# The pause of TensorE in the second unit of every segment: the wait moved one matmul forward, ahead of the next one

## The chip, the cores and the metric

The kernel runs on one core of a Trainium2 chip. The metric is the time of one execution on the device in microseconds (us), the median of several runs. Everything is computed in one launch.

## The reference

Two blocks follow one another on 256 tokens of width 2048. Nearly all of the work is in projections, which multiply the activations by weights of 2048 rows.

```python
# first block
h = rmsnorm(x, ln_g); proj = h @ w_in                      # gMLP, delta-rule and cross-attention inputs
out_a = gmlp_spatial_gating(...) * silu(g_z)
out_b = rmsnorm(gated_delta_rule(q, k, v, g, beta)) * silu(d_z)
out_c = cross_attention(c_q, memory keys, memory values) * silu(c_z)
x = rmsnorm(x + concat(out_a, out_b, out_c) @ w_out, final_g)
# second block
h = rms_norm(x, gain); proj = h @ w_in_2
merged = sigmoid(g_a) * (stick_breaking(q_a, k_a, v_a) @ w_branch_a) \
       + sigmoid(g_b) * (forgetting(q_b, k_b, v_b) @ w_branch_b)
x = x + merged @ w_out_2
# expert layer: query, top-16 product keys per head, softmax gates, 16384 experts
x = x + sum_k gate_k * gelu(expert_u[id_k] . h) * expert_v[id_k]
out = rms_norm(x, final_gain)
```

The kernel computes the expert layer densely: in 8 chunks of 2048 experts an "up" projection by `expert_u`, a product with a dense table of gates, and a "down" projection by `expert_v`.

## The kernel before

**Units.** All projections are cut into 460 units. A unit is one block of 2048 x 128 weights (1 MB) against all 256 tokens, accumulated in one PSUM bank. It is done in two halves (h = 0, 1) of 8 tiles of 128 rows each. To keep float32 accuracy, weights and activations are split into an upper and a lower part, and each tile takes three matmuls: upper weights by upper activations, upper weights by lower activations, and lower weights by upper activations. A half is therefore three groups of 8 matmuls, and a unit is 48 matmuls with 48 weight loads. Every one of them has the shape 128x128 by 128x256.

**Who makes what.** SyncE loads the weights (`raw`, a ring of 4 units). ScalarE makes the upper part `whi` of a half (line 427), GpSimd the lower part `wlo` (line 404), TensorE multiplies (all matmuls are recorded at line 1345), ScalarE or VectorE takes the result out of PSUM. `whi` and `wlo` have 4 slots, one for each half: ScalarE may convert a half once TensorE has finished the half four before it. The activations are `xhi`, `xlo` (or `bhi`, `blo`; in the down projections `hid_upper`, `hid_lower`). The semaphores are `hi_ready`, `lo_ready` (a half is converted), `pe_half` (TensorE has finished a half) and `evac` (a bank is free).

**Segments.** TensorE's program is written as segments of 4 to 24 units, 34 in all. The first two units of a segment are written out, and the rest are in a loop of two units. Between some segments other work stands (transposes, attention, sums for the norms). Eight units at the start and the 16 units of the up projection of chunk 2, between which the gate table is built, are written without segments.

**The pause.** In the second unit of each segment (`paused` is true for j = 1) the last of the first 8 matmuls of half 0 increments a semaphore `beat` when it is finished, and TensorE itself waits for that semaphore a little later. Nobody else uses `beat`. Where `fresh` is set for this unit, which is so only in the paired segment of the branches, the group with `wlo` comes before the one with the lower activations; elsewhere the lower activations come first.

Of the kernel before, what the change touches and what calls it, by code (L numbers as in the profile page):

```python
# [29 lines left out]
HALF = KT // 2  # L30
# [78 lines left out]
def program(nc, ap, out, g_dram):  # L109
    ctx = ExitStack()  # L110
    with ctx:
# [193 lines left out]
        conv_used, beat = sem("conv_used"), sem("beat")  # L305
# [1037 lines left out]
        def _(pe):  # L1343
# [3 lines left out]
            beats = [0]  # L1347


            def pause(k, z):  # L1350
                if k == HALF - 1:
                    z.then_inc(beat, 1)
                    beats[0] += 1
                elif k == 0:
                    pe.wait_ge(beat, beats[0])

            def unit_body(u, j, hi, lo, par, paired=False, fresh=None, between=None, paused=False):

                s0 = (2 * j) % 4
                o = unit_ps[:, j % 2, :]
                if not (isinstance(par, int) and par == 0):
                    pe.wait_ge(evac[j % 2], par)
                for h in range(2):
                    def tile(k):
                        return k + HALF * (j % 2) if paired else k + HALF * h

                    def upper_x(k):
                        if fresh is not None and k % 4 == 0:  # L1370
                            pe.wait_ge(*fresh(tile(k) // 4)[0])

                    def lower_x(k):
                        if fresh is not None and k % 4 == 0:
                            pe.wait_ge(*fresh(tile(k) // 4)[1])

                    oo = o[:, h * S:(h + 1) * S] if paired else o[:, 0:S]
                    opens, closes = paired or h == 0, paired or h == 1
                    pe.wait_ge(hi_ready, u * 2 + (2 * j + h + 1))
                    for k in range(HALF):  # L1380
                        upper_x(k)
                        z = mm(oo, whi[:, s0 + h, k, :], hi[:, tile(k), :], start=opens and k == 0, stop=False)
                        if paused and h == 0 and k == HALF - 1:
                            pause(k, z)

                    def with_lower_x(stop):
                        for k in range(HALF):
                            lower_x(k)
                            z = mm(oo, whi[:, s0 + h, k, :], lo[:, tile(k), :], start=False, stop=stop and k == HALF - 1)
                            if paused and h == 0 and k == 0:  # L1390
                                pause(k, z)
                        return z

                    def with_lower_w(stop):
                        pe.wait_ge(lo_ready, u * 2 + (2 * j + h + 1))
                        for k in range(HALF):
                            z = mm(oo, wlo[:, s0 + h, k, :], hi[:, tile(k), :], start=False, stop=stop and k == HALF - 1)
                        return z

                    if fresh is not None:  # L1400
                        with_lower_w(False)
                        z = with_lower_x(closes)
                    else:
                        with_lower_x(False)
                        z = with_lower_w(closes)
                    z.then_inc(pe_half, 1)

                    if between is not None and h == 0:
                        between()
# [73 lines left out]
            for t in range(TT):  # L1483
                for h in range(XA_HEADS):
                    z = tr(psf[:, 1024 + (t * 4 + h) * P:1024 + (t * 4 + h + 1) * P], mvf[:, h, t * P:(t + 1) * P])
# [10 lines left out]
            for h in range(XA_HEADS):  # L1496
                for t in range(TT):
                    n = 2 * h + t
                    z = mm(psf[:, 1024 + n * S:1024 + (n + 1) * S], cq[:, h, t * P:(t + 1) * P], mk[:, h, :])
# [3 lines left out]
            for h in range(XA_HEADS):  # L1503
                for m in range(TT):
                    for t in range(TT):
                        z = tr(psf[:, 1024 + (2 * h + m) * S + t * P:1024 + (2 * h + m) * S + (t + 1) * P],
                               xa_p[:, 2 * h + t, m * P:(m + 1) * P])
# [4 lines left out]
            for h in range(XA_HEADS):  # L1512
                for m in range(TT):
                    z = mm(psf[:, h * S:(h + 1) * S], mvt[:, m, h, :], xa_pt[:, h, m, :], m == 0, m == TT - 1)
# [4 lines left out]
            for g in range(GROUPS):  # L1519
                z = mm(psf[:, 1024:1024 + S], ones, gv[:, g, :], g == 0, g == GROUPS - 1)  # L1520
# [9 lines left out]
            for t in range(TT):  # L1530
                for x, m in enumerate((C64_LE, C64_GT)):
                    z = mm(psf[:, 768 + (2 * t + x) * 8:768 + (2 * t + x + 1) * 8], c(m), gbt[:, t, 0, :])
            z.then_inc(sg("gsum_mm"), 1)
            pe.wait_ge(sg("ln_sq"), 1)
            for g in range(GROUPS):
                z = mm(psf[:, 1536:1536 + S], ones, vsq[:, g, :], g == 0, g == GROUPS - 1)
# [3 lines left out]
            for g in range(GROUPS):  # L1540
                for t in range(TT):
                    z = tr(psf[:, 2048 + (2 * g + t) * P:2048 + (2 * g + t + 1) * P], gv[:, g, t * P:(t + 1) * P])
# [4 lines left out]
            for g in range(GROUPS):  # L1547
                for t in range(TT):
                    o = psf[:, 1024 + (2 * g + t) * P:1024 + (2 * g + t + 1) * P]
                    z = mm(o, vt[:, g, t, :], wst[:, g, :])  # L1550
# [30 lines left out]
            for n in range(16):  # L1581
                z = tr(ps_b[:, n * P:(n + 1) * P], qkv[:, 8 + n // 2, (n % 2) * P:(n % 2 + 1) * P])
            z.then_inc(sg("k_t"), 1)
            pe.wait_ge(sg("exp_row"), 1)
            for n in range(16):
                kk = qkv[:, 8 + n // 2, (n % 2) * P:(n % 2 + 1) * P]
                z = mm(ps_a[:, n * P:(n + 1) * P], kk, kk)
# [4 lines left out]
            for n in range(16):  # L1592
                z = tr(ps_b[:, n * P:(n + 1) * P], qkv[:, 16 + n // 2, (n % 2) * P:(n % 2 + 1) * P])
            z.then_inc(sg("v_dt"), 1)
            pe.wait_ge(sg("kk_out"), 1)
            for n in range(16):
                sl = slice((n % 2) * P, (n % 2 + 1) * P)
                z = mm(ps_a[:, n * P:(n + 1) * P], qkv[:, 8 + n // 2, sl], qkv[:, n // 2, sl])
# [291 lines left out]
```

## Time and profile before

| | |
|---|---|
| median of 3 runs | 3000.95 us (2997.36 to 3005.54) |
| profiled execution, own time | 3004.29 us |
| its span, first to last instruction | 3002.5 us |
| TensorE matmuls busy | 2906.8 us, 97% |
| TensorE weight loads busy | 2865.0 us, 95% |
| GpSimd busy | 2289.1 us, 76% |
| ScalarE busy | 1312.0 us, 44% |
| VectorE busy | 1063.2 us, 35% |
| mean granted TensorE clock | 0.987 of full speed |

The busy times come from one profiled execution. Matmuls overlap one another in the records (one begins before the last has ended), so the rate of TensorE is read from the distance between starts and not from busy time.

### The profile page before, as it was taken

How to read it: one execution, taken by the hardware profiler on the slowest of the kernel's cores; microseconds unless marked ns; L12 is line 12 of the kernel's file. 1: busy time of each engine (PE TensorE's matmuls, PEld its weight loads, DVE VectorE, ACT ScalarE, POOL GpSimd, SP SyncE). 2: the span in 40 equal slices, each digit the busy share in tenths (PEclk: the TensorE clock that was granted, in tenths of full speed). 3: DMA queues.
4: the chain of work that ended last, by engine and by line, in shares of the span. 5: the costliest groups of instructions: out<-in, count | busy, mean ns of one | idle time of the engine just before them, and what ended most of it. 6: DMA issues, size and time to landing. Idle time of an engine off the chain costs nothing.

```text
span 3002.5 us, 58955 instructions
## 1 busy us (share of the span) xinstructions
PE 2906.8 (97%) x24182; PEld 2865.0 (95%) x24182; DVE 1063.2 (35%) x1558; ACT 1312.0 (44%) x1547; POOL 2289.1 (76%) x925
## 2 busy tenths in 40 slices
PE   7999979999999988999999999999999999999998
PEld 7999979899999987999999999999999999999998
DVE  6113365353000025225698981403104040033322
ACT  6355542554534343444443664343433334333333
POOL 6787730588878852888799548888888888889986
PEclk9999989999999998999999999999999999999999
DMA  6445410344545530555454555564564645655553
GB/s 241 169 175 184 162 62 0 113 176 175 194 169 196 182 140 31 193 195 183 156 182 177 215 224 210 182 219 173 192 215 180 224 168 196 219 192 205 211 188 118
DMA packets 85829, 524.37 MB, mean 175 GB/s; under 512 B 8672, under 2 KB 23136, under 8 KB 24544
## 3 DMA queue, kind: packets, MB, share of 16 engines
q1 hardware_dynamic: 68400, 489.38, 45.5%
q10 hardware_dynamic: 17328, 33.56, 3.0%
q8 instruction: 75, 1.23, 0.2%
q14 instruction: 26, 0.21, 0.0%
HBM read 504.03 MB, written 18.87 MB: 174 GB/s over the span
## 4 chain that ended last, share of the span: by engine, by line
PE 51%; POOL 23%; issue 20%; DVE 5%; POOLq 0%; ACT 0%; DVEq 0%; ACTq 0%
PE banks L1345 51%; POOL wlo L404 23%; DVE oh L1273 2%; DVE oh L1269 1%; DVE hidden L1283 1%; POOLq L403 0%; DVE T L800 0%; PE banks L1455 0%; DVE hid_lower L1316 0%; DVE dec L1007 0%; POOLq L398 0%; DVE picks L1254 0%; DVE at__97 L1015 0%; DVE qkv L967 0%; ACT expr L605 0%
## 5 line engine op out<-in xcount | busy, mean ns | idle before, releaser
L404 POOL TENSOR_TENSOR wlo<-raw,whi 128x1024 fp32r<-128x1024 f32 x920 | 2284.4, 2504 | 661.6 <-ACT whi L427 660.7
L427 ACT ACTIVATE whi<-raw 128x1024 fp32r<-128x1024 f32 x916 | 943.0, 1055 | 763.2 <-PE banks L1345 755.8
L1345 PE MATMUL banks<-xhi,whi 128*128 128x256 f32 x4928 | 681.8, 281 | 7.1 <-ACT xhi L508 7.0
L1345 PE MATMUL banks<-xhi,wlo 128*128 128x256 f32 x4928 | 678.4, 280 | 6.2 <-POOL wlo L404 6.2
L1345 PE MATMUL banks<-xlo,whi 128*128 128x256 f32 x4928 | 682.6, 281 | 1.9 <-DVE xlo L807 1.9
L1345 PEld LDWEIGHTS banks<-xhi,whi 128*128 128x128 f32 x4928 | 622.1, 189 | 9.3 <-issue 7.8
L1345 PEld LDWEIGHTS banks<-xlo,whi 128*128 128x128 f32 x4928 | 623.4, 189 | 5.8 <-DVE xlo L807 2.5
L1345 PEld LDWEIGHTS banks<-xhi,wlo 128*128 128x128 f32 x4928 | 620.9, 189 | 7.6 <-POOL wlo L404 7.6
L878 DVE TENSOR_TENSOR X<-banks,X 128x256 f32 (+1 forms) x112 | 47.5, 424 | 768.9 <-PE banks L1345 768.9
L1345 PE MATMUL banks<-hid_lower,whi 128*128 128x256 f32 x2048 | 285.5, 282 | 2.4 <-DVE hid_lower L1316 2.4
L1345 PEld LDWEIGHTS banks<-hid_lower,whi 128*128 128x128 f32 x2048 | 261.1, 190 | 3.7 <-DVE hid_lower L1316 2.6
L453 ACT ACTIVATE hidden<-banks 128x256 f32 (+1 forms) x128 | 49.4, 386 | 401.0 <-PE banks L1345 400.8
L1345 PE MATMUL banks<-hid_upper,whi 128*128 128x256 f32 x1536 | 213.1, 282 | 0.0
L1345 PE MATMUL banks<-hid_upper,wlo 128*128 128x256 f32 x1536 | 212.2, 281 | 0.0
L1345 PEld LDWEIGHTS banks<-hid_upper,whi 128*128 128x128 f32 x1536 | 195.4, 190 | 0.0
L1345 PEld LDWEIGHTS banks<-hid_upper,wlo 128*128 128x128 f32 x1536 | 194.3, 189 | 0.0
L1273 DVE TENSOR_SCALAR oh<-banks,sel 128x128 f32<-128x128 f32 x256 | 84.2, 398 | 0.0
L1310 DVE TENSOR_TENSOR hidden<-hidden,gch 128x1024 f32<-128x1024 f32 x28 | 59.2, 2114 | 60.7 <-PE banks L1345 60.7
L1345 PE MATMUL banks<-bhi,wlo 128*128 128x256 f32 x512 | 70.9, 281 | 0.7 <-POOL wlo L404 0.7
L1345 PE MATMUL banks<-bhi,whi 128*128 128x256 f32 x512 | 71.2, 282 | 0.0
L1345 PE MATMUL banks<-blo,whi 128*128 128x256 f32 x512 | 71.1, 281 | 0.0
L1345 PE MATMUL banks<-oh,oh 128*128 128x128 f32 x512 | 64.3, 282 | 4.0 <-DVE oh L1273 3.2
(352 smaller groups left out, 2156.8 us busy)
## 6 DMA issues: line engine op xcount, KB each, us to landing
raw<-in_w_exp SPq DMA_DIRECT2D x256, 1024.0 KB, 4.8
raw<-in_w_in SPq DMA_DIRECT2D x132, 1024.0 KB, 4.8
raw<-in_w_out SPq DMA_DIRECT2D x32, 1024.0 KB, 4.8
raw<-in_w_br SPq DMA_DIRECT2D x16, 1024.0 KB, 4.8
raw<-in_w_q SPq DMA_DIRECT2D x16, 1024.0 KB, 4.8
gates<-gst ACTq DMA_DIRECT2D x16, 1024.0 KB, 4.7
gch<-gates ACTq DMA_DIRECT2D x7, 2048.0 KB, 12.8
raw<-in_w_kv SPq DMA_DIRECT2D x8, 1024.0 KB, 9.5
```

The costliest lines, as they stand in the source:

```text
L404: pool.tensor_tensor(wlo[:, s, :, :], raw[:, j, h * HALF:(h + 1) * HALF, :], whi[:, s, :, :].bitcast(F32), ALU.subtract).then_inc(lo_ready, 1)
L427: act.activation(whi[:, (2 * j + h) % 4, :, :], raw[:, j, h * HALF:(h + 1) * HALF, :], ACT.Copy).then_inc(hi_ready, 1)
L453: act.activation(dst[:, bass.ds(i * RING + j, 1), :], unit_ps[:, j % 2:j % 2 + 1, 0:S], func).then_inc(evac[j % 2], 1)
L878: return dve.tensor_tensor(blk(X, i, j), unit_ps[:, j % 2:j % 2 + 1, 0:S], blk(X, i, j), ALU.add)
L1269: dve.tensor_tensor(oh2[:, b8:b8 + 8, :], iota.unsqueeze(1).broadcast_to([P, 8, P]), row.unsqueeze(2).broadcast_to([P, 8, P]), ALU.is_equa ...
L1273: dve.tensor_scalar(oh1[:, b, :], iota, col(0), col(2), ALU.is_equal, ALU.mult).then_inc(sg("oh"), 1)
L1283: dve.tensor_tensor(h, h, gst[:, g16 % 2, 0:KT, :], ALU.mult).then_inc(sg("gated_first"), 1)
L1310: dve.tensor_tensor(h4, h4, gch[:, :, ks, :].rearrange("p g a n -> p a g n"), ALU.mult).then_inc(sg("gates_used"), 1)
L1345: return nc.tensor.matmul(o, lhsT, rhs, start=start, stop=stop, **k)
```

## The change

The wait for `beat` is placed directly behind the matmul that increments it, ahead of the very next matmul. Before, one more matmul was issued in between. Nothing else differs; no other engine's program changes.

```diff
-            def pause(k, z):
-                if k == HALF - 1:
-                    z.then_inc(beat, 1)
-                    beats[0] += 1
-                elif k == 0:
-                    pe.wait_ge(beat, beats[0])
+            def pause(z):
+                z.then_inc(beat, 1)
+                beats[0] += 1
+                pe.wait_ge(beat, beats[0])
...
                     for k in range(HALF):
                         upper_x(k)
                         z = mm(oo, whi[:, s0 + h, k, :], hi[:, tile(k), :], start=opens and k == 0, stop=False)
                         if paused and h == 0 and k == HALF - 1:
-                            pause(k, z)
+                            pause(z)
 
                     def with_lower_x(stop):
                         for k in range(HALF):
                             lower_x(k)
                             z = mm(oo, whi[:, s0 + h, k, :], lo[:, tile(k), :], start=False, stop=stop and k == HALF - 1)
-                            if paused and h == 0 and k == 0:
-                                pause(k, z)
                         return z
```

TensorE's program at the pause of an ordinary segment (the up projection of chunk 0), before the change. A row is one matmul or several alike, out <- moving operand, weights; the first two rows are the 8 upper by upper matmuls.

```order
L1345 MATMUL banks<-xhi,whi 128x256 [waits hi_ready,evac1]
L1345 MATMUL banks<-xhi,whi 128x256 x7
L1345 MATMUL banks<-xlo,whi 128x256
L1345 MATMUL banks<-xlo,whi 128x256 [waits beat]
L1345 MATMUL banks<-xlo,whi 128x256 x6
L1345 MATMUL banks<-xhi,wlo 128x256 [waits lo_ready]
L1345 MATMUL banks<-xhi,wlo 128x256 x7
```

The same place of the changed kernel:

```order
L1345 MATMUL banks<-xhi,whi 128x256 [waits hi_ready,evac1]
L1345 MATMUL banks<-xhi,whi 128x256 x7
L1345 MATMUL banks<-xlo,whi 128x256 [waits beat]
L1345 MATMUL banks<-xlo,whi 128x256 x7
L1345 MATMUL banks<-xhi,wlo 128x256 [waits lo_ready]
L1345 MATMUL banks<-xhi,wlo 128x256 x7
```

The wait has moved from the second to the first of the eight matmuls behind the one that it waits for. 33 of the 34 pauses look like this one.

The one in the paired segment of the branches, before the change:

```order
L1345 MATMUL banks<-xhi,whi 128x256 [waits lin_hi]
L1345 MATMUL banks<-xhi,whi 128x256 x3
L1345 MATMUL banks<-xhi,wlo 128x256 [waits lo_ready]
L1345 MATMUL banks<-xhi,wlo 128x256 x7
L1345 MATMUL banks<-xlo,whi 128x256 [waits lin_lo2]
L1345 MATMUL banks<-xlo,whi 128x256 [waits beat]
L1345 MATMUL banks<-xlo,whi 128x256 x2
```

And the same place of the changed kernel:

```order
L1345 MATMUL banks<-xhi,whi 128x256 [waits lin_hi]
L1345 MATMUL banks<-xhi,whi 128x256 x3
L1345 MATMUL banks<-xhi,wlo 128x256 [waits lo_ready,beat]
L1345 MATMUL banks<-xhi,wlo 128x256 x7
L1345 MATMUL banks<-xlo,whi 128x256 [waits lin_lo2]
L1345 MATMUL banks<-xlo,whi 128x256 x3
```

Here nine matmuls stood between the increment and the wait, and now none does.

## Rows read from the trace of the kernel before

**Rows 1.** The page: busy time (share of the span) of each engine

```profile
PE 2906.8 (97%) x24182; PEld 2865.0 (95%) x24182; DVE 1063.2 (35%) x1558; ACT 1312.0 (44%) x1547; POOL 2289.1 (76%) x925
```

**Rows 2.** Two stretches of 76 us, matmuls of line 1345 (busy, count; loads; clock; DMA)

```profile
1190.00:1266.00 76.00, 76.00 (x673) 76.00 (x672) 1.00 0.57 205
1284.00:1360.00 76.00, 76.00 (x648) 76.00 (x647) 1.00 0.55 199
```

**Rows 3.** Matmuls in order of time about two pauses (start, length, group)

```profile
76.20 1.07 PE L1345 MATMUL banks<-xhi,whi 128*128 128x256 f32 x8
77.10 1.31 PE L1345 MATMUL banks<-xlo,whi 128*128 128x256 f32 x8
78.25 1.11 PE L1345 MATMUL banks<-xhi,wlo 128*128 128x256 f32 x8
79.19 1.11 PE L1345 MATMUL banks<-xhi,whi 128*128 128x256 f32 x8
...
1997.42 0.40 PE L1345 MATMUL banks<-hid_upper,whi 128*128 128x256 f32 x2
...
1997.66 0.72 PE L1345 MATMUL banks<-hid_lower,whi 128*128 128x256 f32 x3
...
1997.88 0.19 PEld L1345 LDWEIGHTS banks<-hid_lower,whi 128*128 128x128 f32 x1
```

**Rows 4.** The same about the pause at 230.62 us

```profile
230.62 1.30 PE L1345 MATMUL banks<-xlo,whi 128*128 128x256 f32 x8
231.76 1.07 PE L1345 MATMUL banks<-xhi,wlo 128*128 128x256 f32 x8
```

**Rows 5.** The same about two waits for GpSimd's weights

```profile
1362.44 1.10 PE L1345 MATMUL banks<-bhi,whi 128*128 128x256 f32 x8
1363.44 1.19 PE L1345 MATMUL banks<-bhi,wlo 128*128 128x256 f32 x8
1364.47 1.07 PE L1345 MATMUL banks<-blo,whi 128*128 128x256 f32 x8
...
1540.55 1.10 PE L1345 MATMUL banks<-xlo,whi 128*128 128x256 f32 x8
1541.86 1.20 PE L1345 MATMUL banks<-xhi,wlo 128*128 128x256 f32 x8 [0.21 <-POOL wlo L404]
1542.89 1.07 PE L1345 MATMUL banks<-xhi,whi 128*128 128x256 f32 x8
```

**Rows 6.** First and last of 16 stretches behind a pause, and their sum

```profile
77.30:93.30 16.00, 16.00 (x136) 15.96 (x135) 1.00 0.62 222
...
1816.50:2988.30 1171.80, 1171.80 (x9928) 1170.05 (x9928) 1.00 0.55 195
sum 2013.10, PE 2013.10 PEld 2010.57; mean PE 125.82 PEld 125.66
```

**Rows 7.** The up projections of chunks 0 and 1, and what VectorE waits for there

```profile
1469.90:1541.40 71.50, 71.50 (x608) 71.50 (x607) 1.00 0.47 162
1563.20:1637.60 74.40, 74.40 (x633) 74.32 (x631) 1.00 0.52 185
...
DVE gs L1252 <- ACT picks L743: 6.4, 1, 6.4
```

**Rows 8.** GpSimd in an up projection while VectorE gates, and who needs it

```profile
1907.77 18.98 POOL L404 TENSOR_TENSOR wlo<-raw,whi 128x1024 fp32r<-128x1024 f32 x6 [3.13 <-ACT whi L427]
...
1929.52 3.38 POOL L404 TENSOR_TENSOR wlo<-raw,whi 128x1024 fp32r<-128x1024 f32 x1
...
1933.59 1.11 PE L1345 MATMUL banks<-xhi,wlo 128*128 128x256 f32 x8
```

**Rows 9.** Three stretches behind a pause that are not slow: line 1345 alone

```profile
1183.10:1267.80 84.70, 83.74 (x739) 83.55 (x739) 1.00 0.53 186
231.50:245.50 14.00, 14.00 (x126) 14.00 (x125) 1.00 0.40 135
303.50:317.90 14.40, 14.40 (x129) 14.40 (x128) 1.00 0.42 148
```

## The prediction

> **What bounds the kernel now.** I began with the page. TensorE's matmuls are busy 97% of the span, GpSimd 76%, VectorE 35% and ScalarE 44% [rows 1]. So the question is what sets TensorE's rate, and busy time doesn't tell it, since matmuls overlap in the records. I went to windows and counted matmuls in two stretches of 76 us in which TensorE neither waits nor does anything but line 1345. In the one it issues 673, in the other 648, at the same granted clock of 1.00 and with the same shape [rows 2]. That is 112.9 ns and 117.3 ns from start to start: **TensorE has two pitches**, 4.4 ns apart. In the timeline they can be told by the length of a group of eight, 1.07 us against 1.10 to 1.11 [rows 3, 4].
>
> Then I looked where the pitch changes. At 77.10 us a pause stands in a fast stretch: the group ahead of it is 1.07 long, those behind it are 1.11 long and 0.94 apart [rows 3]. So the present pause makes the pitch slow. At 1997.66 it is slow before and behind. Of the 33 ordinary pauses two end in the fast pitch, those at 230.62 [rows 4] and 302.73. Between pauses the pitch stays what it is, over all turns of the loop: the stretch from 1816.5 to 2988.3 us is slow from end to end (9,928 matmuls), and its twelve pauses change nothing [rows 6].
>
> The waits for other engines do the opposite. At 1363.44 and 1541.86 TensorE waits in the middle of a slow stream for GpSimd's weights, and goes on in the fast pitch: the groups behind are 1.07 long [rows 5]. I went through the timeline for all places between 70 and 1807 us at which TensorE, at full clock and between two matmuls of this shape, waited for over 0.15 us for another engine. Leaving out two after which it waited again within four matmuls, there are 13, six of them in a slow stream, and the stream behind every one is fast; two of them are in [rows 5].
>
> What tells the two kinds apart is what the change alters. At 1997 the last upper matmul, the one that counts up, starts at 1997.54 (0.12 behind the 1997.42 of the row of two). The load that waits for it starts at 1997.88, 0.34 later. In between one matmul has started alone at 1997.66, and the next is at 1997.88 and the third at 1998.10, so there are two starts 0.22 apart in a row [rows 3]. A matmul is 0.28 us long, so the lone one is still in the array when TensorE goes on. At a wait for another engine there is one gap ahead of the first matmul and one of 0.22 behind it.
>
> **The change part by part.** (1) *The pitch.* At an ordinary pause nothing is issued between the increment and the wait, so the load goes 0.34 us behind the start of the counted matmul, which is 0.28 long: the array has been empty for some 0.06. This is a single gap, as at the 13 waits for others. The shortest of those gaps is at 1363.44, 1.00 behind 1362.44, of which seven pitches are 0.82, so 0.18; at 1541.86 it is 1.31 - 0.82 = 0.49 behind the start ahead, and both turn fast [rows 5]. 0.34 lies between. I take the fast pitch behind every pause. Sixteen stretches behind pauses are slow now, between 77.3 and 2988.3 us, 2013.1 us together, all with TensorE at work throughout [rows 6]. At 673 for 648 matmuls they take 1 - 648/673 = 3.71% less: **74.8 us**.
>
> (2) *Two stretches more*, the up projections of chunks 0 and 1, are slow too: 71.5 + 74.4 us, 3.71% of which is 5.4 us. Beside them VectorE selects the experts. Its chain doesn't wait for TensorE there but once, 6.4 us for ScalarE's `picks`, whose place is behind TensorE's units [rows 7]. So up to 6.4 us can be passed on, but TensorE also waits for GpSimd there (as at 1541.86) at moments that VectorE's work sets. Bounds 0 and 5.4; I take half, **2.7 us**. The projection of chunk 2 has no pause and goes by VectorE's table: nothing.
>
> (3) *The pause itself.* Now it costs 78.25 - 77.10 = 1.15 less the 0.94 of a group, 0.21 us [rows 3]. Then it costs 0.34 - 0.11 = 0.23 ahead of the first matmul, and 1364.47 - 1363.44 = 1.03 less 0.91, 0.12, for the group behind [rows 5]: 0.35. That is 0.14 more at 33 pauses, 4.6 us. The 34th, in the branches, waits for nothing today, since nine matmuls of 0.11 stand in between; it gets the whole 0.35. Together **5.0 us** lost.
>
> (4) *The other engines.* In a fast stream a half takes 24 x 112.9 = 2.71 us in place of 2.82. GpSimd must make one `wlo` in this time. Its mean is 2289.1 / 925 = 2.47 [rows 1], but beside VectorE's gating six took 18.98 us, 3.16 each, and the lead melts: the one that starts at 1929.52 ends at 1932.90, 0.69 ahead of 1933.59, where TensorE wants it [rows 8]. Over eight such halves TensorE gains 8 x 0.11 = 0.9, and the ring of four starts GpSimd 0.4 nearer to TensorE's need (88 matmuls of 4.4 ns less lie between the half that frees the slot and the first use of the new one). So the lead of 0.69 becomes a wait of about 0.6 us, in five up projections (chunks 3 to 7): **3.0 us** lost, bounds 0 and 10. A wait of that kind itself ends in the fast pitch. Weights of 1 MB in 5.42 us are no new load: the fast stretch in [rows 2] moved 205 GB/s and TensorE didn't wait.
>
> Sum: 74.8 + 2.7 - 5.0 - 3.0 = 69.5 us. The profiled execution took 3004.3, which gives 2934.8. The median is 3.3 lower, so I predict **2931 us**. With the bounds of (2) and (4) alone: 3001 - 74.8 - 5.4 + 5.0 = 2926, and 3001 - 74.8 + 5.0 + 10 = 2941.
>
> **The rivals.** (A) *The pitch is what it was*: the pause that TensorE makes for its own semaphore is always the same number of steps behind its own matmul, where the waits for others fall anywhere; that may be why 31 of 33 end slow, whatever is issued between. Then only the price (3) is left: 3001 + 5.0 = 3006 us. For it: the regularity of the outcome, and that at 1363.44, too, a matmul was in the array, and the pitch turned fast nevertheless. Against it: no single gap in this stream ended slow. The Trainium skill ("TensorE: Matmul & The Clock Gate", section "Back-to-back issue gap") gives for the isolated gap of a warm matmul N / 2.4 + 2.5 ns, an estimate of 109.2 ns here, by N and the clock alone, whatever ran before. By that rule the pause can change no pitch, and rival A is what is left. The trace disagrees, with 112.9 and 117.3 ns at one clock and one shape.
>
> (B) *A lottery*: the short gap turns some pauses fast, others slow. With half of them 74.8 + 2.7 shrinks to 39: about 2966, anywhere from 2945 to 2990.
>
> (C) *Another engine takes over*: GpSimd or the loads can't hold 5.42 us a unit over 1,170 us, and most of the gain goes into waits. 3001 - 20 = 2981. Against it: GpSimd's mean of 2.47 us is well under the 2.71 that a fast half leaves it.
>
> (D) *The empty restart makes the pitch slow everywhere*, slower than before. Three stretches behind pauses are fast today, 84.7, 14.0 and 14.4 us [rows 9], the first of them in the branches where the pause now waits for nothing. Turned slow they take 673/648 - 1 = 3.86% more, 4.4 us, beside the 5.0 of (3): 3001 + 9.4 = 3010 us. It is over 0.3% (9 us) only if all three turn. Against it: the 13 waits.
>
> **How the numbers follow.** Chances: forecast 0.72, B 0.09, C 0.04, A 0.08, D 0.07. A measurement of this kernel tells about 0.3% (9 us) from no change. Forecast, B and C are faster: 0.85. A is the same, 0.08. D is slower, 0.07. The likeliest case's own range is 2922 to 2944, the bounds above with some room. The range runs from 2921 to 2980, which takes in most of B and leaves out A, D and the ends.
>
> **What would show it.** In the changed kernel's trace a pause has one start about 0.34 behind the counted matmul, one 0.22 later, and then groups 1.07 long and 0.91 apart. A window of 76 us in the long stretch counts 673 matmuls, not 648. TensorE's waits for GpSimd's `wlo` appear in the up projections of chunks 3 to 7, about 0.6 us each. The last stretch lasts some 1,133 us instead of 1,172. I am wrong if groups behind the pause stay 1.10 long: then A, or D if those in the branches turn as well. If they are 1.07 long and the time is still over 2950, TensorE's waits must name the engine of C.

## The result, and the profile after

The changed kernel takes **2983.39 us**, the median of 6 runs (2972.43 to 2985.73). The kernel before, run beside it, takes 3002.11 us (6 runs, 2997.36 to 3005.54). The ratio is 0.9923, with a 95% interval of 0.9907 to 0.9938: 18.7 us faster, where I had forecast 70. The profiled execution took 2985.31 us, with a span of 2983.5. Where executions of one kernel, the one before included, lie over 1.5% apart, the ratios in this document compare the faster ones alone.

I looked first at the page. TensorE is busy for 97% again, and GpSimd's mean is what it was, 2288.4 / 925 = 2.47 us [rows 1], so no other engine has become the bound.

```profile
PE 2887.4 (97%) x24182; PEld 2839.2 (95%) x24182; DVE 1080.4 (36%) x1558; ACT 1313.1 (44%) x1547; POOL 2288.4 (77%) x925
...
L404 POOL TENSOR_TENSOR wlo<-raw,whi 128x1024 fp32r<-128x1024 f32 x920 | 2283.7, 2503 | 643.9 <-ACT whi L427 642.3
```

Then the windows of line 1345, as in [rows 2]: stretch, its length, matmuls busy and counted, loads busy and counted, granted clock, DMA share, GB/s. Here are five in the order of the program.

```profile
1284.00:1360.00 76.00, 76.00 (x673) 76.00 (x672) 1.00 0.57 207
1816.50:1904.00 87.50, 87.50 (x741) 87.50 (x741) 0.99 0.61 216
...
1997.50:2085.50 88.00, 88.00 (x750) 88.00 (x748) 1.00 0.61 214
...
2178.00:2263.00 85.00, 85.00 (x752) 85.00 (x751) 1.00 0.62 221
2266.00:2353.00 87.00, 87.00 (x741) 87.00 (x740) 1.00 0.50 181
```

1284 to 1360 counts 673 now, where it was 648 [rows 2]. 2178 to 2263 has 113.0 ns a matmul and is fast; 1997 to 2085 has 117.3 and is slow, with 117.4 behind it from 2266 on. Both pitches are still there, and they now change places within the expert layer, which was slow from end to end [rows 6]. (A window also counts the matmuls that its ends cut, so these quotients are a little too small. The starts of single matmuls lie 113.3 and 117.8 ns apart; the difference of 4.4 ns stays.)

The timeline shows where they change (start, length, group). First the pause at 1907.35, second the one at 1995.02:

```profile
1905.25 1.11 PE L1345 MATMUL banks<-xhi,wlo 128*128 128x256 f32 x8
1906.19 1.10 PE L1345 MATMUL banks<-xhi,whi 128*128 128x256 f32 x8
1907.35 1.19 PE L1345 MATMUL banks<-xlo,whi 128*128 128x256 f32 x8
1908.38 1.07 PE L1345 MATMUL banks<-xhi,wlo 128*128 128x256 f32 x8
...
1992.98 1.07 PE L1345 MATMUL banks<-hid_lower,whi 128*128 128x256 f32 x8
1993.89 1.07 PE L1345 MATMUL banks<-hid_upper,whi 128*128 128x256 f32 x8
1995.02 1.21 PE L1345 MATMUL banks<-hid_lower,whi 128*128 128x256 f32 x8
1996.06 1.10 PE L1345 MATMUL banks<-hid_upper,wlo 128*128 128x256 f32 x8
```

At 1907.35 groups of 1.10 and 1.11 stand ahead and 1.07 behind: slow becomes fast. At 1995.02 the same kind of pause turns fast into slow. I call it *drained*, since nothing is issued between the counted matmul and the wait. So it goes at 32 of the 33 ordinary pauses: **the drained pause turns the pitch over**, 16 times slow to fast and 16 times fast to slow. The 33rd, at 1815.82, falls in a stretch where the granted clock is half and matmuls are 213 to 214 ns apart, so that nothing can be said of the pitch ahead; the stream behind it is slow. The pause in the branches, at 1190.34, also makes a fast stream slow (until a wait for VectorE at 1192.60). In the expert layer the ordinary ones at full clock are at 1907, 1995, 2085, 2175, 2263, 2354, 2441, 2532, 2619, 2710, 2797 and 2888 us, and all but one strictly alternate. The exception is at 2175: the stretch behind 2085 had been made slow again, by a wait for GpSimd.

```profile
2110.40 1.07 PE L1345 MATMUL banks<-xlo,whi 128*128 128x256 f32 x8
2111.49 1.21 PE L1345 MATMUL banks<-xhi,wlo 128*128 128x256 f32 x8
2112.53 1.11 PE L1345 MATMUL banks<-xhi,whi 128*128 128x256 f32 x8
```

TensorE comes to this group 0.18 late (1.09 for 0.91) and goes on slow. That is a wait for another engine of the size of those in [rows 5], with the opposite end. Its gap is 290 ns from start to start; at 1933.04 the same kind of wait, with a gap of 286 ns, left a fast stream fast.

**The gain adds up.** From 1816.5 to 2970 the slow stretches are now 90.5 (from the start to 1907), 90 (from 1995), 63.5 (2111.5 to 2175) and four of 91 (from 2263, 2441, 2619 and 2797), 608 us in all; the other 545 are fast. At 3.86% that is 21.1 us. Twelve pauses at 0.14 more take 1.7 of it, two waits for GpSimd 0.3: 19.1. Measured: TensorE takes up `picks` at 1654.98 (was 1655.41), and the last sum for the norm at 2969.37 (was 2988.32), so 18.5 us were won between them. Ahead of it 2.0 us had been won by 1102 us, and 0.4 were left at 1655. What took them back in between I haven't followed wait by wait.

### The profile page after: what moved, and what is told of

It reads as the page before. It is cut to its first block, busy times and chain, and to the rows that moved or that the text cites. A ratio compares the mean times of both kernels' runs of the same rounds, so it can differ in the third digit from the quotient of the medians.

```text
span 2983.5 us, 58956 instructions
## 1 busy us (share of the span) xinstructions
PE 2887.4 (97%) x24182; PEld 2839.2 (95%) x24182; DVE 1080.4 (36%) x1558; ACT 1313.1 (44%) x1547; POOL 2288.4 (77%) x925
## 4 chain that ended last, share of the span: by engine, by line
PE 51%; POOL 23%; issue 21%; DVE 5%; POOLq 0%; ACT 0%; DVEq 0%; ACTq 0%
PE banks L1345 51%; POOL wlo L404 23%; DVE oh L1273 2%; DVE oh L1269 1%; DVE hidden L1283 1%; POOLq L403 0%; DVE T L800 0%; PE banks L1451 0%; DVE hid_lower L1316 0%; DVE dec L1007 0%; POOLq L398 0%; DVE picks L1254 0%; DVE at__97 L1015 0%; ACT expr L605 0%; ACT L499 0%
## 5 line engine op out<-in xcount | busy, mean ns | idle before, releaser
L1345 PE MATMUL banks<-hid_lower,whi 128*128 128x256 f32 x2048 | 279.4, 279 | 2.9 <-DVE hid_lower L1316 2.4
```

The lines of the kernel that those rows point to most:

```text
L1345: return nc.tensor.matmul(o, lhsT, rhs, start=start, stop=stop, **k)
```

## The experiments

"S" and "F" are the slow and the fast pitch, so FS is a pause that goes from fast to slow, and FF one that leaves a fast stream fast. Gaps in ns are read from the starts of single matmuls.

### No pause at all, and the pause in some segments

```diff
# e_none: segment()
-  unit_body(u0, j, ..., between if j == 0 else None, j == 1)
+  unit_body(u0, j, ..., between if j == 0 else None)
# e_last_up3
+  unit_body(u0, j, ..., between if j == 0 else None, j == 1 and u0 <= first_unit("up", 3))
# e_two: the drained pause in both halves of the unit
-  if paused and h == 0 and k == HALF - 1:
+  if paused and k == HALF - 1:
```

> No segment pauses at all. Seen in the changed kernel's trace: every one of its pauses turned the pitch over, fast (113 ns a matmul) to slow (118) and slow to fast. Theory T (a drained pause turns the pitch over; nothing within a segment does but a wait for another engine): without pauses each long stretch keeps the pitch with which it begins, so I expect no change of pitch between 1817 us and the end, and a time that hangs on that one pitch: about 3000 us if it is slow (12 pauses of 0.2 us less than before, 3 us), about 2957 if it is fast. Rival R (the pitch wanders by itself and a pause has nothing to do with it): changes of pitch inside the long stretch without any gap.

> The changed kernel with its last pause in the up projection of chunk 3; the 11 segments behind it have none. In the changed kernel's trace that pause (1907 us) turned slow into fast. Theory T: from there on every matmul stays fast, save for short waits for GpSimd; against the changed kernel five slow segments of 90 us turn fast (5 x 90.7 x 3.77% = 17 us) and 11 pauses of 0.35 go (4 us): 2984 - 21 = 2963 us. Rival R (a stream falls back into the slow pitch after a while unless paused): slow groups reappear without a pause and the time is at or over 2984. Rival C (at a lasting fast pitch GpSimd or the loads take over as the bound): TensorE's waits for wlo add up to over 5 us and the time is near 2975.

> Two drained pauses in the paused unit, one in each half, 24 matmuls apart. Theory T: the second undoes the first, so every segment ends with the pitch that it began with and the long stretch from 1817 us has one pitch but for 24 matmuls in each segment: about 3010 us if slow (13 further pauses of 0.35 us), about 2968 if fast; in the trace each pair reads fast-slow-fast or slow-fast-slow. Rival R2 (what counts is the place, the second unit's first half, and the state that follows there): a mix as in the changed kernel, near 2990.

Without a pause the kernel takes 2941.97 us (2936.19 to 2942.91), against 3002.58 beside it: ratio 0.980 (0.9783 to 0.9816), under the 2957 that was expected for a fast stretch. The expert layer is fast from 1813 us on:

```profile
1820.00:1896.00 76.00, 76.00 (x673) 76.00 (x673) 1.00 0.51 184
2000.00:2076.00 76.00, 76.00 (x673) 76.00 (x672) 1.00 0.51 181
```

So a kernel in the fast pitch does come near my 2931, though this one pays for no pause. It also has the waits for GpSimd that I had forecast in the fast stream: five, each a gap of 375 ns (0.26 us more than a pitch), at 1908.6, 2083.1, 2257.5, 2432.0 and 2606.4 us, and here each ends fast.

With pauses up to the up projection of chunk 3 alone, the median of five is 2954.72, four of them being 3002.27, 2953.54, 2954.72 and 2954.61 (the fifth, at a mean granted clock of 0.746, is told below). The expectation was 2963. The execution of 3002.27 was the profiled one:

```profile
1906.91 1.10 PE L1345 MATMUL banks<-xhi,whi 128*128 128x256 f32 x8
1908.07 1.20 PE L1345 MATMUL banks<-xlo,whi 128*128 128x256 f32 x8
1909.11 1.07 PE L1345 MATMUL banks<-xhi,wlo 128*128 128x256 f32 x8
...
1932.68 1.07 PE L1345 MATMUL banks<-xlo,whi 128*128 128x256 f32 x8
1933.76 1.21 PE L1345 MATMUL banks<-xhi,wlo 128*128 128x256 f32 x8
1934.81 1.11 PE L1345 MATMUL banks<-xhi,whi 128*128 128x256 f32 x8
...
1940.00:2950.00 1010.00, 1010.00 (x8578) 1010.00 (x8577) 1.00 0.56 200
```

The last pause turns the stream fast at 1908.07. A wait for `wlo` at 1933.76, a gap of 290 ns, turns it slow, and as nothing stops TensorE any more it stays slow for 1,010 us (117.7 ns a matmul). One wait of 0.18 us costs about 38 (1,010 us at 3.8%). With two drained pauses in a unit ten executions fall apart into 2951 to 2981 (five) and 3002 to 3015 (five); the eleventh, the profiled one, had a clock of 0.763, and the median of all is 3001.98. So one program has several times. Both sums of the expectation (2968 and 3010) have executions near them, but which pause did what can't be seen: the profiled execution ran at a lower clock throughout.

### Six kinds of pause side by side

```diff
# e_kinds: units 2 to 4 (2 to 8 in the expert layer) of a segment written out,
# a kind for each half from a shuffled table, 318 trials
+ if kind == 1 and k == HALF - 2 or kind in (0, 2, 3) and k == HALF - 1: count(z)
...
+ if kind in (4, 5):
+     count(mm(banks[:, 5, 0:w], whi[...], hi[:, tile(HALF - 1), 0:w], start=True, stop=True))
+ if kind in (0, 1, 3, 4, 5): hold()
...                                       # behind the next matmul, k == 0
+ if kind == 3: count(z)
+ if kind in (2, 3): hold()
```

Kind 0 is the changed kernel's pause, 2 that of the kernel before, 1 the same a matmul earlier, 3 two drained pauses with a lone matmul between them, 4 and 5 a drained pause behind an extra matmul of 64 or 128 columns, into a bank that nobody reads (in the last chunks alone).

> A probe, read from the trace, not from its time: units behind the first are written out (three in each segment, seven in the expert layer), and behind the first eight matmuls of each half stands one of six pauses in a shuffled order. 0: drained, as in the changed kernel. 1: the wait for the matmul before the last, so one gap but the array not empty. 2: as in the kernel before (one matmul between). 3: drained, then one matmul alone, then drained again. 4 and 5: an extra matmul of 64 or 128 columns into an unused bank is waited for, which only shifts the moment of going on (a few tens of ns). Theory T as 'a drained pause turns over': kinds 0, 4 and 5 turn over both ways, 3 leaves the pitch, 1 and 2 mostly end slow. Rival P (the moment of going on, counted from the stream's own start, decides, a few ns either way): each kind has its own fixed outcome for a fast and for a slow stream ahead, 4 and 5 unlike 0; one kind may end fast from both. Rival E (my forecast's: an empty array ends fast): kinds 0, 3, 4, 5 end fast from both.

> The probe of six kinds of pause once more, to be read from its trace. Theory Q: its table is either the one seen (kind 0 turns over, kinds 1 and 2 make fast slow, kind 3 keeps, kinds 4 and 5 end fast), cell by cell, or another one that is as clear-cut, in which kinds 1 and 2 leave fast fast. Rival V: the same kinds with mixed outcomes.

> The probe a third time. Theory Q: the table of setting 1 or that of setting 2 comes again. Rival: a third table, so that the setting is a quantity with more than two values.

| kind | e_kinds, chip 9 | e_kinds_again, chip 3 | e_kinds_third, chip 6 |
|---|---|---|---|
| 0 drained | SF 54, FS 49 | FF 65, SS 26, SF 12 | SF 54, FS 49 |
| 1 one between, a matmul earlier | FS 37, SS 14, SF 2 | FF 34, SF 19 | FS 36, SS 14, SF 2 (one at half clock) |
| 2 one between (before) | FS 23, SF 30 | FF 28, SF 25 | FS 23, SF 30 |
| 3 drained twice | FF 29, SS 23, SF 1 | FS 46, SF 7 | FF 29, SS 23, SF 1 |
| 4 and 64 columns | FF 15, SF 13 | FS 23, SS 5 | FF 15, SF 13 |
| 5 and 128 columns | FF 17, SF 10, SS 1 | FF 17, SF 8, SS 3 | FF 17, SF 10, SS 1 |

(These are all 318 trials of each; the expectations count one fewer of kind 2.)

Three things follow. In the first column kind 0 turned the pitch over 103 times in 103, so the alternation of the changed kernel is no chance. What a kind does hangs on the pitch it meets: under kind 0 the counted matmul stands 333 to 334 ns ahead of the restart in a fast stream, 336 to 338 in a slow one. And it hangs on **something that differs between executions**: on chip 3 the same program gave another table, with 334 to 335 ns from fast and 337 to 339 from slow, about 1 ns later. The third, on chip 6, gave the first table again. I call the first *setting 1* and the second *setting 2*. The times were 3073.70, 3061.06 and 3072.76 us.

From a slow stream kind 1 mostly ended slow in the first table and kind 2 always fast, though the kernel before, whose pause is kind 2, ended slow 17 times of 19. Single starts settle this. A slow stream repeats itself every three matmuls: the steps are 117.3, 117.7 and 118.3 ns on average. Call it place 0 where the longest step lies directly ahead of the last regular matmul before the gap (under kind 1, of the counted one), place 1 and 2 where it lies one or two matmuls further ahead. Then all 16 traces that have pauses at full clock can be read together, those of the runs told further down among them. Ten show setting 1 (the first trace of the kernel before, the changed kernel three times, two of the probes, e_last_up3, e_extra64, e_few64, e_both_kinds), six setting 2 (e_before_again, e_cycle, e_extra64_again, e_kinds_again, e_wide_all, e_wide_twice). The end and the number of pauses met in a slow stream, at places 0, 1, 2:

| kind | setting 1 | setting 2 |
|---|---|---|
| 0 | F 52, F 102, F 8 | S 18, S 8, F 12 |
| 1 | S 28, none, F 4 | F 7, F 8, F 4 |
| 2 | S 19, F 63, F 2 | F 19, F 11, F 10 |
| 3 | S 10, S 36, F 2 | none, F 2, F 5 |
| 4 | F 8, F 24, F 2 | S 10, F 2, F 9 |
| 5 | S 8, F 20, none | F 12, F 8, S 6 |

No cell has two ends, in 539 pauses, nor has any kind two ends from a fast stream in one setting (780 pauses). **Within a setting the kind, the pitch ahead and the place in the cycle of three fix the outcome.** Since each trace is put into a setting by what its pauses do, this shows that two tables are enough, not what chooses between them. It also explains [rows 6]: in the kernel before, pauses in the expert layer are 768 matmuls apart, a multiple of three, so the slow stream is met at place 0 each time and stays slow (17 of 17 in the whole trace), and the pauses at 230.62 and 302.73, which ended fast, met it at place 1.

### The kernel before and the changed one on other chips

> The kernel before, unchanged, for a second trace and more times. Beside the last runs it took 2935 us in three executions of seven and 2997 to 3011 in the other four, while it had taken 2997 to 3007 in all 19 seen until then; and in the trace of the run with the shifted pause every pause met in the fast pitch left it fast, which no pause of that kind had done in the earlier traces. Theory Q: each execution has from its start to its end one of two settings; in the one a pause of this kind ends slow when it meets a fast stream, in the other it ends fast. Then the times here fall into two groups, 2935 and 3003, nothing in between, and a trace of an execution at 2935 shows fast to fast at every pause. Rival V (the outcome of each pause is drawn anew): times spread between, and fast-to-fast and fast-to-slow pauses mix in one trace.

> The changed kernel, unchanged. Theory Q: two groups of times: 2984 in executions of the first setting (pauses turn the pitch over), and where the second setting leaves a fast stream fast, some 2936 (the kernel before there, 2935, and some 0.15 us more at 33 pauses, less what the slow starts of segments give). Rival V: a spread between 2940 and 2990.

> The changed kernel a third time, beside the kernel before. Theory Q: the kernel before is at 3003 or 2935 by its setting, the changed one, whose drained pause turned the pitch over in both traces seen, between 2955 and 2985; so the ratio is 0.992 or 1.011 by the setting of the kernel before, and not by the change. If the probe's second table (drained pause keeps fast fast) comes up for this kernel, it is near 2936.

Unchanged, the kernel before has two times. These are its 82 executions (the profiled one before the change, at 3004.29, makes one more):

| where | executions | us |
|---|---|---|
| the runs of the result | 6 | 2997 to 3006 |
| chip 9 | 13 | 2997 to 3007 |
| chip 3, first occasion | 4 and 3 | 2997 to 3011 and 2934 to 2935 |
| chip 3, second occasion | 28 | 2926 to 2944 |
| chip 6 | 11 | 2996 to 3012 |
| chip 0 | 2 and 15 | 3005 to 3008 and 2930 to 2940 |

Nothing lies between 2944 and 2996. The trace of one at 2934.45 us (e_before_again) shows why: its own pause there never makes a fast stream slow. Of 32 ordinary pauses 23 are FF and 9 SF. Here are its pause at 1876, and a window of the stretches behind it:

```profile
1875.59 1.10 PE L1345 MATMUL banks<-xhi,whi 128*128 128x256 f32 x8
1876.53 1.30 PE L1345 MATMUL banks<-xlo,whi 128*128 128x256 f32 x8
1877.67 1.07 PE L1345 MATMUL banks<-xhi,wlo 128*128 128x256 f32 x8
...
2000.00:2076.00 76.00, 76.00 (x671) 75.86 (x671) 1.00 0.52 180
```

The group of 1.30 is the old pause of [rows 3]; behind it stands 1.07 and stays. The changed kernel on that chip takes 2975.74 us (6 runs, 2955.34 to 2984.47) beside 2937.65: **slower, ratio 1.0109** (1.0076 to 1.0141). All 32 ordinary pauses that its trace shows turn the pitch over there too (18 FS, 14 SF). The one at 131.78 stands in a fast stream, which is slow behind it:

```profile
130.65 1.07 PE L1345 MATMUL banks<-xhi,whi 128*128 128x256 f32 x8
131.78 1.21 PE L1345 MATMUL banks<-xlo,whi 128*128 128x256 f32 x8
```

On chip 6, where the kernel before takes 3006.21, it takes 2980.44 (2976.64 to 2987.60), ratio 0.9919 (0.9900 to 0.9937), turned over again. So the changed kernel has about one time, 2970 to 2988 in 16 of 18 executions, and the sign of the change hangs on which of its two times the kernel before has.

> The kernel without pauses once more, beside the two above on the same chip: 2942 us as before if its states are the same in each execution, up to 45 us more in executions in which the long stretch begins slow.

> The kernel without pauses, a third time. It took 2936 to 2943 in four executions and 2943 to 2987 in four others. Nothing sets its pitch but the waits for other engines and the ends of other work; theory Q gives no single time, but a spread between 2935 and 2990, lower than the changed kernel in the mean (2983).

Nor is the kernel without pauses safe. On chip 3 it took 2942.58, 2984.24, 2987.40 and 2974.68; on chip 6 the median of six is 2976.46 (2941.05 to 2983.36), ratio 0.9879 (0.9839 to 0.9919). The profiled execution on chip 6 had become slow and stayed so; the row is the expert layer, 117.7 ns a matmul:

```profile
1816.50:2905.00 1088.50, 1088.50 (x9245) 1088.50 (x9244) 1.00 0.56 198
```

### Pauses made longer by a small matmul

```diff
# e_extra64 (e_few64: in ten segments alone)
-  if paused and h == 0 and k == HALF - 1:
-      pause(z)
+  if paused and h == 0 and not paired:      # behind the loop over k
+      pause(mm(o[:, S:S + 64], whi[:, s0, HALF - 1, :], hi[:, tile(HALF - 1), 0:64], start=False, stop=False))
# e_wide_all: 128 columns, o[:, S:S + P], in their place
```

The extra matmul writes columns of the bank that nobody reads.

> The changed kernel, but in each of its 33 ordinary pauses TensorE first issues one matmul more, of 64 columns into an unused part of the bank, and waits for that one; the pause of the branches is left out. In the probe this pause ended in the fast pitch from both (28 of 28), where the plain drained one turned the pitch over (103 of 103). Theory P (the moment of going on decides, not that the array is empty): all 33 end fast, slow groups are left only between the end of other work and the next pause and where chunk 2 builds its table; against the run without pauses 21 us of slow pitch shrink to some 5 and 33 x 0.35 = 12 us of pauses come: about 2938 us. Rival T (any drained pause turns over): the same alternation as in the changed kernel, near 2990.

> No pauses but ten of the kind with the extra 64 columns: in the first long segments behind other work and in four of the expert layer. Theory P: the stream is fast from each of them on, so of the 4842 slow matmuls of the run without pauses (21 us) some 2800 turn fast (12 us) for 10 x 0.35 = 3.5 us: about 2933 us where the run without pauses takes 2942. Rival (those segments' slow time was covered by other engines): at 2945, slow groups gone but waits in their place.

> The pauses that wait for an extra matmul of 64 columns, once more: 2933, 2944, 2945 and 2989 us so far. If this pause ended fast in each setting, all executions would be near 2935; the 2989 speaks against it. Theory Q: two groups of times again, one near 2935 and one at 2985 or above, the latter in executions of the setting whose trace hasn't been seen for this kernel.

> Each ordinary pause waits for an extra matmul of 128 columns. In the three probes this pause met a fast stream 51 times and left it fast each time, in both settings; a slow one it turned fast 28 times of 33. Theory Q: near 2935 us in either setting, the whole expert layer fast, with 33 pauses of 0.4 us in it. Rival (a setting not seen yet, as for the pause of 64 columns, which was good in the one setting and bad in the other): 2960 to 2990.

With 64 columns at all 33 places the kernel took 2932.73, 2989.00, 2944.21 and 2944.84 us on chip 3. In the trace of the first all 33 end fast, and the expert layer is fast throughout:

```profile
1816.50:2905.00 1088.50, 1087.81 (x9578) 1086.46 (x9577) 1.00 0.57 202
```

On the second occasion on the same chip it took 2988.62 (2984.20 to 2991.85), ratio 1.0171 (1.0155 to 1.0187) to the kernel before at 2937.65, and 16 of the same pauses turned fast into slow (12 SF, 5 SS). At ten places it took 2938.59 to 2980.72 (median 2954.54) where 2933 was expected. A version that was best in one execution was the worst in another.

With 128 columns, on chip 0, eleven executions lie within 2935.47 and 2945.63 (median 2940.19), ratio 1.0022 (1.0012 to 1.0031) to the kernel before, of whose 17 executions there the two at 3005 to 3008 are left out of the comparison. In its trace no pause makes a fast stream slow (25 FF, 7 SF, 1 SS; behind one of the FF the clock is half for 3 us). At 1883.77 the stream ahead is fast (the group of nine has the extra matmul) and stays so:

```profile
1881.68 1.07 PE L1345 MATMUL banks<-xhi,wlo 128*128 128x256 f32 x8
1882.59 1.13 PE L1345 MATMUL banks<-xhi,whi 128*128 128x256 f32 x9
1883.77 1.19 PE L1345 MATMUL banks<-xlo,whi 128*128 128x256 f32 x8
1884.80 1.07 PE L1345 MATMUL banks<-xhi,wlo 128*128 128x256 f32 x8
```

It is the only pause that kept fast fast in both settings of the probe, too (17 of 17 each). But the kernel as a whole was seen only where the kernel before was mostly at 2935; whether it stays at 2940 where that one takes 3000 wasn't tried.

### Where the old pause stands, and two pauses together

```diff
# e_cycle, on the kernel before: the old pause counted on the 6th, 7th or 8th matmul by turns
+  turns[0] += 1
+  return HALF - 3 + (turns[0] - 1) % 3
# e_both_kinds: ten places, half 0 the old pause, half 1 the one with 128 columns
+  if paused and h == 0: count(z)
+  if paused and h == 1: count(mm(o[:, S:S + P], ..., hi[:, tile(HALF - 1), 0:P], ...)); hold()
# e_wide_twice: ten places, the one with 128 columns in both halves
+  if paused and k == HALF - 1 - h: pause(mm(o[:, S:S + P], ..., hi[:, tile(HALF - 1), 0:P], ...))
```

> The pause of the kernel before (one matmul between the counted one and the wait), but counted on the 6th, 7th and 8th matmul by turns, so that each stands 769 or 766 matmuls behind the one before it, not 768, in the long segments. Theory P, refined by the probe: a slow stream repeats itself every three matmuls, and 768 is a multiple of three, so the kernel before meets it at the same point each time, where going on ends slow; one matmul later in the cycle it ended fast 21 times of 21. So fast and slow should alternate in the long stretch as in the changed kernel, and the time come out near 2984 us. Rival (the kind of pause decides: a lone matmul in between ends slow): as before, 3002 us, the long stretch slow throughout.

> Pauses at ten places only, two in the same unit, 24 matmuls apart: first the one of the kernel before (one matmul between), then one that waits for an extra matmul of 128 columns. The two tables of the probe, setting 1 (first run) and setting 2 (second run): in setting 1 the first of them ends slow or fast and the second ended fast 27 times of 28; in setting 2 the first ended fast 52 of 52 and the second kept a fast stream fast 17 of 17. Theory Q: with both, the stream is fast behind the pair in either setting, so all executions lie near 2938 us, whatever the setting. Rival (more than two settings, or places between them): some executions at 2960 to 2990.

> Two such pauses 23 matmuls apart in ten segments only and none elsewhere, so that a slow stream that the first doesn't turn is met by the second at another point of its cycle of three. The pair before it failed because it always met the slow stream at one point. Theory Q: fast from each of the ten places on, near 2940 us in either setting. Rival: slow stretches behind both pauses of a pair, 2960 or more.

e_cycle took 2932.18 and 2936.89 us, and its trace has no pause that makes a fast stream slow: it fell in setting 2, like the three executions at 2935 of the kernel before beside it, and so says nothing on the slow pauses of setting 1, for which it was made.

e_both_kinds took 2968.29 on chip 6 (2963.68 to 2979.74), ratio 0.9885 (0.9863 to 0.9908). Where the old pause left a fast stream (four of ten) the second kept it; where it left a slow one (six) the second left it slow, all six times. Two places, the old pause first:

```profile
253.38 1.10 PE L1345 MATMUL banks<-xhi,whi 128*128 128x256 f32 x8
254.32 1.30 PE L1345 MATMUL banks<-xlo,whi 128*128 128x256 f32 x8
255.46 1.07 PE L1345 MATMUL banks<-xhi,wlo 128*128 128x256 f32 x8
...
257.55 1.19 PE L1345 MATMUL banks<-xlo,whi 128*128 128x256 f32 x8
258.58 1.07 PE L1345 MATMUL banks<-xhi,wlo 128*128 128x256 f32 x8
...
826.09 1.07 PE L1345 MATMUL banks<-xhi,whi 128*128 128x256 f32 x8
827.00 1.31 PE L1345 MATMUL banks<-xlo,whi 128*128 128x256 f32 x8
828.15 1.10 PE L1345 MATMUL banks<-xhi,wlo 128*128 128x256 f32 x8
...
830.31 1.21 PE L1345 MATMUL banks<-xlo,whi 128*128 128x256 f32 x8
831.36 1.10 PE L1345 MATMUL banks<-xhi,wlo 128*128 128x256 f32 x8
```

In the probe the same kind 5 turned 10 of 11 slow streams fast. There it met 10 of them at place 1 and the one that stayed slow at place 0; here it stands always the same number of matmuls behind the old pause and met all six at place 0. A pause can't be costed alone, and the expected 2938 was missed. e_wide_twice took 2952.26 (2948.17 to 2962.05), between the 2940 of its theory and the 2960 of its rival, ratio 1.0064 (1.0051 to 1.0078); at two places where the first left the stream slow the second turned it fast.

## Why the prediction was wrong, by its own steps

**Two pitches, kept between gaps: right.** They are 4.4 ns apart at a granted clock of 1.00 in every trace, and fast kernels take 2926 to 2945 us, about where I put this one. The size of the whole term, 74.8 us for sixteen stretches, was near but somewhat high: the kernel before at its other time, no pause of which makes a fast stream slow, is some 65 to 70 us faster than at 3002, where the terms (1), (2) and (4) together said 74.5.

**Step (1), that a drained restart ends fast: wrong, and this is the step that failed.** I wrote that "the array has been empty for some 0.06. This is a single gap, as at the 13 waits for others", and took the fast pitch behind every pause. Of the 33 ordinary ones 16 ended fast, and the drained pause turned the pitch over instead. The two gaps that I had compared are alike in the timeline, and the stream behind them is not. The 13 waits were too few, of many lengths, and no two of them told what a gap of 0.34 does from a *fast* stream and from a *slow* one; I had not asked how it depends on the pitch ahead, nor on the place in it. The changed kernel's own waits at 2111.49 and e_last_up3's at 1933.76 go from fast to slow. The number of gaps is not the cause: kind 0 with one gap made 49 fast streams slow in setting 1, and kind 2 with two made none so in setting 2.

**Step (2), 2.7 us from two more stretches:** not tried here, since both pauses (1469 and 1562) end slow as before; `picks` is taken up 0.4 us earlier. In e_before_again both stretches are fast, and from the first of these pauses to ScalarE's `picks` it is 178.7 us in place of 181.8: 3.1 us won, near the 2.7.

**Step (3), the price: right.** From 1906.19 to 1907.35 is 1.16, less 0.94; from 1907.35 to 1908.38 is 1.03, less 0.91: 0.34 us, forecast 0.35.

**Step (4), waits for GpSimd in five up projections, 3.0 us:** two waits, at 1933.04 and 2111.49, of some 0.17 us. Only part of these segments runs in the fast pitch. In e_none, where all do, there are five as forecast, of 0.26 us in place of 0.6: the term was sized at over twice its price.

**The rivals.** A (no pitch changes, 3006) is refuted, and so is C: GpSimd's mean is what it was and its waits come to 0.3 us. D, that the drained restart makes the pitch slow everywhere, is half of what happens. B, the lottery, had the right number of fast ends and 2966 us with bounds of 2945 and 2990, and the time lies in them. That is luck, for its mechanism wasn't right: the outcome is fixed by the pitch ahead. I had given it 0.09 because I read "single gap or double gap" off the rows as the whole difference, where the old pause's own 31 of 33 slow ends (rival A's regularity) said that an outcome may be a matter of the exact moment.

**What the sum could not have had** is the setting. The time before that I started from, 3001, is one of the kernel's two times; on chip 3 I would mostly have started from 2935, and the change would have cost 38 us (2975.74 against 2937.65) in place of bringing 19.

**Open.** What makes the setting: only a difference of about 1 ns at the restart was seen (no experiment varied anything that might set it), and that the kernel before on chip 3 had both times on one occasion and one of them on the next. That one execution of the changed kernel and one of the probe on chip 3 (18 FS and 14 SF, against 65 FF, 26 SS and 12 SF for the same pause) differ shows that the setting isn't fixed by the chip alone. The executions of the changed kernel at 2955 and 2960 have no trace. And why a kind at a place ends as it does isn't found: the two tables say what happens, not why. Nor is it known why there are two pitches.

## What to carry to other kernels

Before a pause or a wait is credited with time, count matmuls in equal windows where TensorE never waits: if two counts differ at one clock and one shape, the stream has more than one pitch, and an edit that shifts TensorE by nanoseconds can move the time by up to 2% either way (ratios of 0.980 and 1.017 here). Tabulate each outcome by the state that it met, not by its end alone, and try the kernel before itself on several chips before an effect of this size is called a gain: here six runs within 0.3% of one another stood 65 us from the other time of the same program. No placement of the pause that was tried is sure to be fast; of those tried at every segment, the kernel that waits for an extra matmul of 128 columns spread least (2935 to 2946 in eleven executions, on one chip, where the kernel before was no slower in 15 of 17).

## What the runs showed of the hardware

One stream of 128x128 by 128x256 matmuls with a load each runs at 113.3 or at 117.8 ns a matmul, at one granted clock. It held the slow pitch for over 8,500 matmuls without a gap (e_last_up3, 1940 to 2950 us), and the fast one from 1813 to 2940 us in e_none, through five waits. A gap of a few hundred ns can change it in either direction; a drained self-wait of 333 to 338 ns turned it over in 103 of 103 cases in one execution, and one of 334 to 339 ns in 12 of 103 in another. The Trainium skill ("TensorE: Matmul & The Clock Gate", section "Back-to-back issue gap") gives the gap of an isolated matmul by N and the clock, an estimate of 109.2 ns here, and says that in a stream of load and matmul both set the spacing; no trace of this case shows 109.2, and every trace at full clock shows two pitches.

At a lower granted clock the pitch follows the clock. In e_two the clock was 0.75 and then 0.85 (stretch, its length, matmuls, loads, clock, DMA share, GB/s):

```profile
2000.00:2600.00 600.00, 597.00 (x4187) 594.41 (x4186) 0.75 0.47 170
3000.00:3400.00 400.00, 399.53 (x3171) 397.88 (x3170) 0.85 0.53 189
```

That is 142.6 and 126.0 ns of busy time a matmul, and at half clock the steps are 213.3; times the clock, each is about 107 ns. At full clock the same stream needs 113.3 or 117.8, so there it isn't the clock alone that sets the pace. What does, no run shows.

Two single executions of kernels on one core took 3601.22 and 3531.68 us, at a mean granted clock of 0.746 and 0.763, where all others lie between 0.983 and 0.990. The same page (section "Seeing it yourself") tells of a limit to 13/16 of the clock (0.81) and says that one or two busy cores never trip it. With one core of the program at work the clock was lower here twice, and the second, e_two, shows 0.75 and 0.85, not 0.81; what else ran on the chip no trace shows, so the cause stays open.
